# The prompt's first keys, queries and values moved into the last sample's step, small turns spread over the quanta, and h turned one part earlier

## The chip, the core and the metric

One core of one Trainium2 chip runs the whole program. The metric is the device time of one execution in microseconds; lower is better. TensorE does the matmuls and, against an identity, the transposes ("turns"). VectorE and ScalarE read its results out of PSUM, GpSimd and SyncE start transfers.

## What is computed

Two layers, each over 512 prompt rows (one stream) and 128 sample rows (8 streams of 16 rows with 256 cached rows each). From the reference, cut:

```python
z = rmsnorm(h, ln_in) @ w_in
c_q, c_kv, k_r, g_a, u_val, u_gate, g_c = split(z)
q = rmsnorm(c_q, ln_q) @ w_q_b ; ckv = rmsnorm(c_kv, ln_kv) ; kr = rope(k_r)
q_lat = q_nope @ w_uk
o_lat = softmax(q_lat . ckv + q_rope . kr) @ ckv      # 8 heads; prompt: block-causal; samples: with their cache
y_a = rmsnorm((o_lat @ w_uv) * silu(g_a), ln_out_a)
u = u_val * sigmoid(u_gate) ; v = causal_dwconv(u, 31 taps)
y_c = rmsnorm(silu(layernorm(v)) * silu(g_c), ln_out_c)
h = h + concat(y_a, y_c) @ w_out
h = h + sigmoid(rmsnorm(h, ln_pg) @ w_pg) * (p @ w_pe)
```

A final rmsnorm ends the trunk. All is fp32.

## The kernel before

**Tiles and parts.** The rows are five token tiles of 128, t = 0 to 3 the prompt's and t = 4 the samples'. A dense product is made of parts, each a slab of weight rows. A part's weights come as raw pieces (WR); ScalarE's `high(i)` (L937) rounds them to WHI, VectorE's `low(i)` (L1279) forms WLO, what WHI lacks. `high(i)` first waits until TensorE is through with part i-2, whose place it takes. A **quantum** (L583) is one part on one tile: two halves, and each half three matmuls (WHI on the tile's high half, WLO on it, WHI on its low half) into `acc[t]`, the bank of PSUM that the tile has. Each layer has the parts u0 (numbers 0 to 3), zA (4 to 7), u1 (8 to 11), ga (12 to 15), gc (16 to 19), oa0 and oa1 (20 to 23), oc0 and oc1 (24 to 27), pg0 (28 to 31), pg1 (32 to 35).

**Shared banks.** All that isn't a dense product goes through three other banks, S, T and O. `shared_bank_plan` (L99) gives each its users in a fixed order, mostly in turn (`cyc`). TensorE's `fill_wait` (L307) holds a user until the one before it in its bank is drained by ScalarE or VectorE.

**Order.** Each engine's program is written out in order: `tensor_layer` (L527), `scalar_layer` (L918), `vector_layer` (L1266), GpSimd's (L1620) and SyncE's (L447). In a layer TensorE runs u0 (with the turns of the tap weights, of w_uk, of the conv states and of the embeddings in two blocks), zA, u1 with the latents' turns (`turn_latents`, L654) and the samples' queries (`sample_queries` L664, qs0 and qs1; `latent_queries` L673, ql0 and ql1), ga's first part, then eight **sample steps** s (scores, probabilities' turn `flip_probs`, values, the cache's turn `flip_cache` L715). Between those stand halves of ga and gc, as many a step as `FILL` says. Then come the prompt's first keys, queries and value rows, and 32 **units** u (eight heads of four query blocks i; `scores` L794, `values` L805), again with halves from `FILL`. After them follow the dense oa, oc and pg. `NEXT_PART` names the step at whose start ScalarE and VectorE split the next part.

**VectorE's taps.** The convolution's 124 taps a layer (L1346, L1349: one tap over 5 x 128 columns) are dealt out over places by `TAP`; they fill VectorE between drains.

**Around h.** oc0 (24, 25) and oc1 (26, 27) give the two column halves of the new residual H; `onto_residual` (L1527, adds in L1534) waits for `acc[t]` and adds. `flip_half(("h", t, k))` turns H of tile t, half k; ScalarE and VectorE split what is turned (L1289, XLO in L1295), and pg0 needs it.

## Time and profile before

| | |
|---|---|
| median of 3 runs | 858.03 us (857.94 to 858.8) |
| profiled execution | 859.08 us |
| its span, first to last instruction | 857.3 us |
| granted TensorE clock, mean | 0.979 |
| busy: TensorE, VectorE, ScalarE, GpSimd | 791.9, 572.9, 410.4, 67.9 us |
| chain that ended last | PE 84%, ACT 8%, DVE 5%, issue 2%, DMA 1% |

Times in the rows below count from the span's start. PE is TensorE, PEld its weight loads, DVE VectorE, ACT ScalarE, POOL GpSimd. A row of a timeline has the start, the duration of the group of like instructions (x their number), and in brackets the idle time before and who ended it. The granted clock is 1.00 at 2.4 GHz and 0.50 at 1.2 GHz; between those, a stretch has some of both.

### The profile page before, as it was taken

To read this page: it belongs to the slowest core of one execution; us is meant where nothing else is said; L and a number is where in the kernel's file an instruction comes from. 1 tells how busy PE (TensorE), PEld (TensorE's weight loads), DVE (VectorE), ACT (ScalarE), POOL (GpSimd) and SP (SyncE) were. 2 spreads that over 40 slices of the span, in tenths; PEclk is the share of its full clock that TensorE was granted. 3 is DMA by queue.
4 is the path that set the end of the run, shared out by engine and by line. 5 is a ranking of instruction groups with operands and counts; after the bars stand their busy time and mean duration, and the time that the engine had idled before them with its cause. 6 is when DMAs were issued, how large, how long until landed. Compare 5 with 4: busy or idle time off the path is not lost.

```text
span 857.3 us, 10488 instructions
## 1 busy us (share of the span) xinstructions
PE 791.9 (92%) x3782; PEld 612.0 (71%) x3782; DVE 572.9 (67%) x1093; ACT 410.4 (48%) x944; POOL 67.9 (8%) x104
## 2 busy tenths in 40 slices
PE   6999999889998899989999999998999889998992
PEld 5789878556766578868888878774767556886881
DVE  3337968879893885355463687888989478645455
ACT  3655554544345562244365474565334557313544
POOL 5000124000000420000000012210000030000000
PEclk9999999989999999999999999999999999998997
DMA  9522222010000163312172222211000003331203
GB/s 301 175 75 69 69 67 84 25 50 24 5 22 1 35 199 112 124 51 92 55 258 65 74 75 84 55 55 30 21 26 24 1 24 137 117 117 33 92 1 122
DMA packets 40569, 65.26 MB, mean 76 GB/s; under 512 B 7774, under 2 KB 19898, under 8 KB 40502
## 3 DMA queue, kind: packets, MB, share of 16 engines
q1 hardware_dynamic: 37354, 58.45, 21.7%
q0 software_dynamic: 3104, 6.12, 2.5%
q8 instruction: 31, 0.51, 0.2%
q14 instruction: 20, 0.16, 0.1%
q10 hardware_dynamic: 60, 0.02, 0.0%
HBM read 57.86 MB, written 7.17 MB: 76 GB/s over the span
## 4 chain that ended last, share of the span: by engine, by line
PE 84%; ACT 8%; DVE 5%; issue 2%; DMA 1%; SPq 0%; DVEq 0%; ACTq 0%
PE acc L598 18%; PE acc L600 17%; PE acc L599 17%; PE sharedT L532 6%; PE sharedS L802 4%; PE sharedT L791 4%; PE acc L711 4%; PE sharedO L814 3%; ACT JUNK L928 2%; PE sharedT L785 2%; ACT WHI L932 2%; PE sharedO L532 1%; PE sharedS L532 1%; DVE WLO L1285 1%; ACT KH L932 1%
## 5 line engine op out<-in xcount | busy, mean ns | idle before, releaser
L598 PE MATMUL acc<-WHI,XHI 128*128 128x512 f32 (+1 forms) x720 | 311.8, 433 | 11.4 <-DVE H L1534 8.2
L600 PE MATMUL acc<-WHI,XLO 128*128 128x512 f32 (+1 forms) x720 | 280.8, 390 | 0.0
L599 PE MATMUL acc<-WLO,XHI 128*128 128x512 f32 (+1 forms) x720 | 280.4, 389 | 0.0
L1349 DVE SCALAR_TENSOR_TENSOR VT<-UX,CWT,VT 128x640 f32<-128x640 f32 x240 | 211.8, 883 | 5.3
L1285 DVE SCALAR_TENSOR_TENSOR WLO<-WR,GT,WHI 128x512 fp32r<-128x512 f32 (+1 forms) x144 | 100.1, 737 | 104.6 <-ACT WHI L932 104.5
L598 PEld LDWEIGHTS acc<-WHI,XHI 128*128 128x128 f32 x720 | 137.1, 190 | 42.5 <-issue 14.7
L599 PEld LDWEIGHTS acc<-WLO,XHI 128*128 128x128 f32 x720 | 137.2, 191 | 29.1 <-issue 6.0
L600 PEld LDWEIGHTS acc<-WHI,XLO 128*128 128x128 f32 x720 | 136.6, 190 | 27.1
L932 ACT ACTIVATE WHI<-WR,GT 128x512 fp32r<-128x512 f32 (+1 forms) x144 | 94.8, 708 | 114.0 <-PE acc L600 108.8
L932 ACT ACTIVATE PT<-sharedT 128x384 f32<-128x384 f32 (+1 forms) x80 | 35.9, 448 | 76.3 <-PE sharedT L532 76.2
L814 PEld LDWEIGHTS sharedO<-V,PT 128*128 128x128 f32 x320 | 44.2, 191 | 19.5 <-issue 14.6
L802 PE MATMUL sharedS<-KH,QH 128*128 128x128 f32 (+3 forms) x128 | 47.5, 453 | 5.9 <-DVE NBIAS L1403 3.7
L814 PE MATMUL sharedO<-V,PT 128*128 128x128 f32 x320 | 47.5, 279 | 1.4 <-ACT PT L932 1.4
L1120 ACT ACTIVATE SB<-SB,NBIAS 128x384 f32<-128x384 f32 (+1 forms) x80 | 45.5, 569 | 4.6 <-DVE NBIAS L1403 4.6
L928 ACT ACTIVATE JUNK<-H 128x512 bf16<-128x512 f32 (+1 forms) x50 | 40.2, 803 | 8.2 <-DVE H L1499 4.0
L532 PE MATMUL sharedT<-IDENT,SB 128*128 128x128 f32 x208 | 36.4, 275 | 5.4 <-ACT KH L932 4.2
L711 PE MATMUL acc<-WR,PTR 128*128 128x512 f32 x80 | 37.3, 593 | 0.0
L1403 DVE CUSTOM_DVE_ANT_0 SB<-sharedS,MASK 128x128 f32<-128x128 f32 (+1 forms) x64 | 31.0, 485 | 8.3 <-PE sharedS L802 7.8
L791 PE MATMUL sharedT<-CQT,WQ 128*128 128x512 f32 x64 | 33.3, 647 | 1.4 <-ACT KH L932 1.4
L1009 ACT ACTIVATE TH<-acc,HR 128x512 f32<-128x512 f32 x40 | 27.2, 685 | 12.2 <-PE acc L600 9.0
L532 PEld LDWEIGHTS sharedT<-IDENT,SB 128*128 128x128 f32 x208 | 25.0, 141 | 9.8 <-issue 7.8
L1652 POOL TENSOR_TENSOR VT<-VT,CTK 128x512 f32<-128x512 f32 x10 | 13.5, 1347 | 230.0 <-DVE VT L1455 230.0
(191 smaller groups left out, 857.8 us busy)
## 6 DMA issues: line engine op xcount, KB each, us to landing
WR<-in_w_in_dram SPq DMA_DIRECT2D x32, 256.0 KB, 3.0
WR<-in_w_in_dram SPq DMA_DIRECT2D x16, 512.0 KB, 3.6
WR<-in_w_out_dram SPq DMA_DIRECT2D x16, 512.0 KB, 3.7
WR<-in_w_pg_dram SPq DMA_DIRECT2D x16, 512.0 KB, 3.5
WR<-in_w_in_dram SPq DMA_DIRECT2D x8, 416.0 KB, 3.7
residual_spill<-H SPq DMA_DIRECT2D x5, 512.0 KB, 3.4
H<-residual_spill SPq DMA_DIRECT2D x10, 256.0 KB, 3.4
H<-in_x_prompt_dram SPq DMA_DIRECT2D x4, 512.0 KB, 8.1
```

Source lines behind the costliest of these rows:

```text
L532: return nc.tensor.transpose(out, in_, IDENT[0:rows, 0:rows])
L598: mm(out, hi, w_hi, start=(first and k == 0), stop=False)
L599: mm(out, hi, w_lo, start=False, stop=False)
L600: last = mm(out, lo, w_hi, start=False, stop=(final and k == 1))
L711: last = mm(acc[t][:, :], PTR[:, k, P * t:P * (t + 1)], WR[:, j % RAW, k, :], start=(k == 0), stop=(k == 1))
L791: last = mm(bank((l, name))[:, :], WQ[:, k, h, :], CQT[:, k, 0:SEQ], start=(k == 0), stop=(k == 1))
L802: fill_inc(mm(bank((l, name))[:, 0:w], QH[:, h % 2, P * i:P * (i + 1)], KH[:, h % 2, 0:w], start=True, stop=True), (l, name))
L814: last = mm(quad(name)[:, i, :], PT[:, n % 2, j, :], V[:, j, P * (h // 2):P * (h // 2 + 1)], start=(j == 0), stop=(j == i))
L928: av(JUNK[:, 0:src.shape[-1]], src, ACT.Square, scale=scale * n ** -0.5, accum_out=MS[:, col:col + 1]).then_inc(squares, 1)
L932: return av(out, in_, ACT.Copy) if scale is None else av(out, in_, ACT.Copy, scale=scale)
L1285: out = stt(out=WLO[at_k], in0=raw[:, k, :], scalar=gain_column(i, k), in1=WHI[at_k].bitcast(F32), op0=ALU.mult, op1=ALU.subtract)
L1349: ins = stt(out=out, in0=src, scalar=w, in1=out, op0=ALU.mult, op1=ALU.add)
```

## The change

- **h.** TensorE turns half 0 of tile t of H behind oc1's first part instead of its second; VectorE makes low(27) behind the fourth add of oc0 and the low halves of h between the adds.
- **Preparation of the prompt.** keys(0), queries(0) and value rows 0 and 1 stand in sample step 7, between its halves; the values of sample 7, value rows 2 and 3 and the turn of u's last columns stand behind, between four halves called prep. The samples' head outputs (`oa`) come in unit 0. `FILL` gives 4 halves to each sample step and to prep, then 1, 2, 2, 0 to a head's four units. `TAP` follows. In a step, ScalarE and VectorE now split the next part after the gates, not before.
- **Small turns.** Those of w_uk, the states and the embeddings stand one by one behind quanta of parts 2 and 3, those of u's first columns behind quanta of zA's part 2.
- **Latents.** The sample tile's comes first; twelve quanta of u1 run before them, not ten. qs0's matmuls stand behind the third latent, qs1's behind the fifth, ql0's and ql1's two quanta later, the cache's first turn one more quantum later. high(10) and low(10) stand ahead of the latents' scaling.
- **GpSimd** waits in layer 0 for the last tile of x and the last raw piece at the start before it loads the caches.

The functions `turn_small` and `turn_embeddings` are cut into single turns with the same matmuls. The rest of the diff, cut:

```diff
-for _n, _m in enumerate([4, 4, 4, 4, 4, 4, 3, 3] + [1, 1, 2, 2] * HEADS):
+for _n, _m in [*((n, 4) for n in range(NB)), ("prep", 4), *((NB + u, (1, 2, 2, 0)[u % 4]) for u in range(UNITS))]:
...
-    TAP[_n] = _take(3 + _n % 2)
-TAP["turn"] = _take(8)
+    TAP[_n] = _take((3, 3, 4, 4, 4, 4, 3, 3)[_n])
+TAP["turn"] = _take(6)
 for _u in range(UNITS):
-    TAP[NB + _u] = _take(2 + _u % 2)
+    TAP[NB + _u] = _take((3, 3, 4, 1)[_u % 4])
+LATENT_TILES = [TILES - 1, *range(TILES - 1)]
...
-        for t in range(TILES):
+        for t in LATENT_TILES:
             cyc((l, ("small", t)))
-        cyc(*((l, n) for n in ("qs0", "qs1", "ql0", "ql1")))
+            if t == LATENT_TILES[2]:
+                cyc((l, "qs0"))
+            if t == LATENT_TILES[4]:
+                cyc((l, "qs1"))
+        cyc((l, "ql0"), (l, "ql1"))
         order["T"] += [(l, ("c", 0)), (l, ("c", 1))]
...
-            order["T"].append((l, ("p", s)))
-        order["T"] += [(l, ("k", 0)), (l, ("q", 0))]
-        for j in range(4):
-            cyc((l, ("v", j)))
-        cyc(*((l, ("u", 3, part)) for part in range(2)))
-        order["S"].append((l, "oa"))
+            if s < NB - 1:
+                order["T"].append((l, ("p", s)))
+        order["S"] += [(l, ("v", 0)), (l, ("v", 1)), (l, ("s", NB)), (l, ("u", 3, 0))]
+        order["T"] += [(l, ("k", 0)), (l, ("q", 0)), (l, ("p", NB - 1)), (l, ("v", 2)), (l, ("v", 3))]
+        order["O"] += [(l, ("u", 3, 1)), (l, "oa")]
         for u in range(UNITS):
             h, i = divmod(u, 4)
-            order["S"].append((l, ("s", NB + u)))
+            if u:
+                order["S"].append((l, ("s", NB + u)))
...
-            turn_small()
-            for c in (2, 3):
-                for t in range(TILES):
-                    copied_wait(pe, (l, ("x", t, 1)))
-                    quantum("u0", c, t)
-                if c == 2:
-                    turn_embeddings()
+            turn_taps()
+            for t in range(TILES):
+                copied_wait(pe, (l, ("x", t, 1)))
+                quantum("u0", 2, t)
+                if t < 2:
+                    turn_key_weights(t)
+                elif t < 4:
+                    turn_state(t - 2)
+            for t in range(TILES):
+                quantum("u0", 3, t)
+                if t < 3:
+                    turn_embeddings(t)
             for c in range(4):
                 for t in range(TILES):
                     quantum("zA", c, t)
-                if c == 1:
-                    turn_u(0)
-                    turn_u(1)
+                    if c == 2 and t in (1, 3):
+                        turn_u(t // 2)
...
-            for c in range(2):
-                for t in range(TILES):
-                    quantum("u1", c, t)
+            rest = [("u1", c, t) for c in range(4) for t in range(TILES)] + [("ga", 0, t) for t in range(TILES)]
+            def go_on(n):
+                for _ in range(n):
+                    quantum(*rest.pop(0))
+            go_on(12)
             pe.wait_ge(latents_ready, l + 1)
-            for t in range(TILES):
...
                 turn_latents(t)
-                quantum("u1", 2, t)
...
+                go_on(1)
+                if n == 2:
+                    pe.wait_ge(wq_rot, 2 * (l + 1))
+                    pe.wait_ge(wq_in, 32 * (l + 1))
+                    copied_wait(pe, (l, ("small", TILES - 1)))
+                    sample_queries(0)
+            sample_queries(1)
+            go_on(2)
             copied_wait(pe, (l, "uk0"))
             copied_wait(pe, (l, "uk1"))
-            for t in range(TILES):
-                quantum("u1", 3, t)
-                if t == 0:
-                    copied_wait(pe, (l, ("small", TILES - 1)))
-                if t in (0, 2):
-                    sample_queries(t // 2)
+            latent_queries(0)
+            latent_queries(1)
+            go_on(1)
...
-            for t in range(TILES):
-                quantum("ga", 0, t)
-                if t == 1:
-                    latent_queries(0)
-                    latent_queries(1)
-                if t == 2:
-                    flip_cache(0)
-            copied_wait(pe, (l, "ql1"))
-            sample_scores(0)
-            flip_cache(1)
...
-            keys(0)
-            queries(0)
-            sample_values(NB - 1)
-            for j in range(4):
...
-            turn_u(3)
-            fill_wait(pe, (l, "oa"))
-            copied_wait(pe, (l, ("o", NB - 1)))
-            for h in range(HEADS):
-                last = mm(bank((l, "oa"))[:, VH * h:VH * (h + 1)], OL[:, h, :], WKV[:, h, NOPE:P], start=True, stop=True)
-            fill_inc(last, (l, "oa"))
-            for j in range(4):
-                copied_wait(pe, (l, ("v", j)))
+            if l == 0:
+                pe.wait_ge(tables_in, 16 * 2)
+                pe.wait_ge(const_set, 10)
+            flip_cache(0)
+            go_on(2)
+            copied_wait(pe, (l, "ql1"))
+            sample_scores(0)
+            flip_cache(1)
+            go_on(3)
+            for s in range(NB):
+                if s < NB - 1:
+                    sample_scores(s + 1)
+                filler(s, slice(0, 1))
+                if s:
+                    sample_values(s - 1)
+                if s < NB - 2:
+                    flip_cache(s + 2)
+                if s == NB - 1:
+                    value_rows(0)
+                    keys(0)
+                    filler(s, slice(1, 2))
+                    value_rows(1)
+                    queries(0)
+                    filler(s, slice(2, None))
+                else:
+                    filler(s, slice(1, None))
+                if s in (0, 1):
+                    turn_u(2, (s,))
+                pe.wait_ge(p_scaled, NB * l + s + 1)
+                flip_probs(s, PAST + P)
             scores(0)
+            filler("prep", slice(0, 2))
+            sample_values(NB - 1)
+            value_rows(2)
+            filler("prep", slice(2, None))
+            turn_u(3, (0,))
+            value_rows(3)
+            turn_u(3, (1,))
...
                 filler(NB + u, slice(0, 1))
+                if u == 0:
+                    sample_heads()
+                    for j in range(4):
+                        copied_wait(pe, (l, ("v", j)))
...
-                    if c == 1:
+                    if c == 0:
...
+            high(first_i + 10)
             act.wait_ge(rstd_ready, RSTDS * l + 2)
-            for t in range(TILES):
...
-            high(first_i + 10)
-            for t in range(TILES):
...
-                if t == 1:
+                if t == 0:
                     high(first_i + 11)
...
-                if n in NEXT_PART:
-                    high(first_i + NEXT_PART[n])
...
+                if n in NEXT_PART:
+                    high(first_i + NEXT_PART[n])
...
+            low(first_i + 10)
             dve.wait_ge(rstd_ready, RSTDS * l + 2)
...
-                if n in NEXT_PART:
-                    low(first_i + NEXT_PART[n])
...
+                if n in NEXT_PART:
+                    low(first_i + NEXT_PART[n])
...
+                else:
+                    taps(TAP[s][:2])
+                    queries_out(0)
+                    taps(TAP[s][2:])
...
             low(first_i + 26)
             for t in range(TILES):
                 onto_residual("oc0", t)
-            low(first_i + 27)
-            for t in range(TILES):
-                low_half((l, ("h", t, 0)))
+                if t == 3:
+                    low(first_i + 27)
+                if t > 1:
+                    low_half((l, ("h", t - 2, 0)))
+            low_half((l, ("h", 3, 0)))
+            low_half((l, ("h", 4, 0)))
             low(first_i + 28)
...
+                pool.wait_ge(x_in[TILES - 1], 16)
+                raw_wait(pool, RAW - 1)
```

On VectorE at the end of oc0, layer 0: the adds to H, the splits of weights (WLO) and of turned H (XLO). Before:

```order
L1285 SCALAR_TENSOR_TENSOR WLO<-WR,GT,WHI 128x512 x4
L1534 SCALAR_TENSOR_TENSOR H<-acc,RS,H 128x512 x5
L1285 SCALAR_TENSOR_TENSOR WLO<-WR,GT,WHI 128x512 x2
L1295 TENSOR_TENSOR XLO<-sharedS,XHI 128x512
L1295 TENSOR_TENSOR XLO<-sharedT,XHI 128x512
L1295 TENSOR_TENSOR XLO<-sharedO,XHI 128x512
L1295 TENSOR_TENSOR XLO<-sharedS,XHI 128x512
L1295 TENSOR_TENSOR XLO<-sharedT,XHI 128x512
L1285 SCALAR_TENSOR_TENSOR WLO<-WR,GT,WHI 128x512 x2
L1534 SCALAR_TENSOR_TENSOR H<-acc,RS,H 128x512 x5
```

and changed:

```order
L1579 SCALAR_TENSOR_TENSOR H<-acc,RS,H 128x512 x3
L1334 TENSOR_TENSOR XLO<-sharedS,XHI 128x512
L1579 SCALAR_TENSOR_TENSOR H<-acc,RS,H 128x512
L1324 SCALAR_TENSOR_TENSOR WLO<-WR,GT,WHI 128x512 x2
L1334 TENSOR_TENSOR XLO<-sharedT,XHI 128x512
L1579 SCALAR_TENSOR_TENSOR H<-acc,RS,H 128x512
L1334 TENSOR_TENSOR XLO<-sharedO,XHI 128x512
L1334 TENSOR_TENSOR XLO<-sharedS,XHI 128x512
L1334 TENSOR_TENSOR XLO<-sharedT,XHI 128x512
L1324 SCALAR_TENSOR_TENSOR WLO<-WR,GT,WHI 128x512 x2
L1579 SCALAR_TENSOR_TENSOR H<-acc,RS,H 128x512 x5
```

Two XLO now stand between the adds of oc0 and three behind low(27), where before all five followed it.

On VectorE at the samples' queries, layer 0 (WLO is low(11), VT are taps, QH the drains of qs0 and qs1). Before:

```order
L1349 SCALAR_TENSOR_TENSOR VT<-UX,CWT,VT 128x5x128 x6
L1285 SCALAR_TENSOR_TENSOR WLO<-WR,GT,WHI 128x512 x2
L1349 SCALAR_TENSOR_TENSOR VT<-UX,CWT,VT 128x5x128 x8
L1391 TENSOR_TENSOR QH<-sharedT,ROPET 128x8x16 x4
L1349 SCALAR_TENSOR_TENSOR VT<-UX,CWT,VT 128x5x128 x2
L1391 TENSOR_TENSOR QH<-sharedO,ROPET 128x8x16 x4
L1285 SCALAR_TENSOR_TENSOR WLO<-WR,GT,WHI 128x512 x2
```

and changed:

```order
L1388 SCALAR_TENSOR_TENSOR VT<-UX,CWT,VT 128x5x128 x6
L1324 SCALAR_TENSOR_TENSOR WLO<-WR,GT,WHI 128x512 x2
L1388 SCALAR_TENSOR_TENSOR VT<-UX,CWT,VT 128x5x128 x8
L1430 TENSOR_TENSOR QH<-sharedO,ROPET 128x8x16 x4
L1388 SCALAR_TENSOR_TENSOR VT<-UX,CWT,VT 128x5x128 x2
L1430 TENSOR_TENSOR QH<-sharedO,ROPET 128x8x16 x4
L1324 SCALAR_TENSOR_TENSOR WLO<-WR,GT,WHI 128x512 x2
```

The order is as it was; both drains now read bank O, where before the first read T.

On TensorE at the end of u1, layer 0 (QH,OL are the latent queries ql0 and ql1; V and CKR the cache's rows). Before, where u1's last quantum ended two quanta of ga ahead of the first row:

```order
L678 MATMUL sharedS<-QH,OL 128x128 x4
L678 MATMUL sharedT<-QH,OL 128x128 x4
L598 MATMUL acc<-WHI,XHI 128x512
L599 MATMUL acc<-WLO,XHI 128x512
L600 MATMUL acc<-WHI,XLO 128x512
L598 MATMUL acc<-WHI,XHI 128x512
L599 MATMUL acc<-WLO,XHI 128x512
L600 MATMUL acc<-WHI,XLO 128x512
L532 MATMUL sharedT<-IDENT,V 128x128
```

and changed, where the quantum between is u1's last:

```order
L688 MATMUL sharedS<-QH,OL 128x128 x4
L688 MATMUL sharedT<-QH,OL 128x128 x4
L604 MATMUL acc<-WHI,XHI 128x512
L605 MATMUL acc<-WLO,XHI 128x512
L606 MATMUL acc<-WHI,XLO 128x512
L604 MATMUL acc<-WHI,XHI 128x512
L605 MATMUL acc<-WLO,XHI 128x512
L606 MATMUL acc<-WHI,XLO 128x512
L538 MATMUL sharedT<-IDENT,V 128x128
```

The cache's turn stood behind the third quantum of ga and now stands straight behind u1's last.

## Rows read from the trace of the kernel before

**Rows 1.** The page's busy times: us, share of the span, instructions.
```profile
PE 791.9 (92%) x3782; PEld 612.0 (71%) x3782; DVE 572.9 (67%) x1093; ACT 410.4 (48%) x944; POOL 67.9 (8%) x104
```

**Rows 2.** TensorE's timeline: start, us, engine, line, operation; [idle before <-releaser].
```profile
101.47 0.48 PE L598 MATMUL acc<-WHI,XHI 128*128 128x512 f32 x1
102.25 0.40 PE L598 MATMUL acc<-WHI,XHI 128*128 128x512 f32 x1
102.94 0.39 PE L598 MATMUL acc<-WHI,XHI 128*128 128x512 f32 x1
...
104.31 1.95 PE L669 MATMUL sharedO<-CQT,WQ 128*128 128x128 f32 x16
```

**Rows 3.** Waits: engine and line, whom for, us, times, longest us.
```profile
PE acc L598 <- DVE H L1534: 8.2, 2, 4.1
```

**Rows 4.** TensorE's timeline at the end of oc1 of layer 0.
```profile
365.60 0.60 PE L532 MATMUL sharedT<-IDENT,H 128*128 128x128 f32 x4
370.31 0.55 PE L598 MATMUL acc<-WHI,XHI 128*128 128x512 f32 x1 [4.11 <-DVE H L1534]
```

**Rows 5.** VectorE's timeline at the same place.
```profile
368.09 1.41 DVE L1285 SCALAR_TENSOR_TENSOR WLO<-WR,GT,WHI 128x512 fp32r<-128x512 f32 x2 [0.53 <-ACT WHI L932]
...
369.42 3.38 DVE L1534 SCALAR_TENSOR_TENSOR H<-acc,RS,H 128x512 f32<-128x512 f32 x5
```

**Rows 6.** Stretches: length, busy PE PEld DVE ACT POOL, granted clock, DMA share, GB/s.
```profile
158.54:187.85 29.31, 23.12 (x80) 13.40 (x79) 21.66 (x34) 13.61 (x32) 1.11 (x2) 0.83 0.11 33
574.64:598.66 24.02, 19.95 (x80) 11.81 (x79) 19.64 (x32) 13.53 (x32) 1.11 (x2) 0.93 0.08 27
370.31:374.00 3.69, 3.69 (x11) 3.00 (x12) 2.48 (x4) 0.06 (x1) 0.00 (x0) 0.54 0.44 142
781.34:787.00 5.66, 5.66 (x15) 4.52 (x16) 3.18 (x5) 0.60 (x1) 0.00 (x0) 0.50 0.29 93
187.85:253.78 65.93, 64.08 (x311) 44.96 (x311) 58.72 (x110) 26.26 (x72) 0.00 (x0) 1.00 0.05 19
```

**Rows 7.** Timelines of ScalarE, TensorE and VectorE at the start and in u0.
```profile
11.69 1.33 ACT L932 ACTIVATE WHI<-WR,GT 128x512 fp32r<-128x512 f32 x2 [1.64 <-DMA WR<-in_w_in_dram]
...
33.21 0.63 PE L532 MATMUL sharedS<-IDENT,VT 120*128 120x120 f32 x4 [1.01 <-ACT OL L932]
...
34.63 1.35 ACT L932 ACTIVATE WHI<-WR,GT 128x512 fp32r<-128x512 f32 x2
...
36.01 1.42 DVE L1285 SCALAR_TENSOR_TENSOR WLO<-WR,GT,WHI 128x512 fp32r<-128x512 f32 x2 [0.72 <-ACT WHI L932]
```

**Rows 8.** TensorE's timeline: idle times of layer 0.
```profile
62.66 0.33 PE L532 MATMUL sharedT<-IDENT,H 128*128 128x128 f32 x1 [1.71 <-ACT UX L932]
...
89.54 0.50 PE L598 MATMUL acc<-WHI,XHI 128*128 128x512 f32 x1 [1.17 <-DVE WLO L1285]
...
121.03 0.88 PE L751 MATMUL sharedS<-CTK,V 128*128 128x384 f32 x2 [0.78 <-ACT CTK L932]
...
163.85 1.07 PE L785 MATMUL sharedT<-CKVT,WKV 128*64 128x512 f32 x2 [1.41 <-ACT PT L932]
```

**Rows 9.** VectorE's timeline, layer 0: taps, then the drain of qs0.
```profile
96.13 4.56 DVE L1349 SCALAR_TENSOR_TENSOR VT<-UX,CWT,VT 128x640 f32<-128x640 f32 x5
...
103.37 0.88 DVE L1391 TENSOR_TENSOR QH<-sharedT,ROPET 128x128 f32<-128x128 f32 x4
```

**Rows 10.** ScalarE's timeline, layer 0: high(13), then the latent queries.
```profile
109.10 1.34 ACT L932 ACTIVATE WHI<-WR,GT 128x512 fp32r<-128x512 f32 x2 [5.12 <-PE acc L600]
...
112.87 0.79 ACT L932 ACTIVATE V<-sharedS 128x128 f32<-128x128 f32 x4
113.76 0.79 ACT L932 ACTIVATE V<-sharedT 128x128 f32<-128x128 f32 x4
```

**Rows 11.** TensorE's timeline: the turn of unit 1's probabilities.
```profile
187.85 0.41 PE L532 MATMUL sharedT<-IDENT,SB 128*128 128x128 f32 x2 [0.35 <-ACT KH L932]
```

**Rows 12.** The page's costliest groups: busy, mean ns; idle before.
```profile
L932 ACT ACTIVATE PT<-sharedT 128x384 f32<-128x384 f32 (+1 forms) x80 | 35.9, 448 | 76.3 <-PE sharedT L532 76.2
```

More of the change, by code:

```diff
@@ L1179, in scalar_layer @@
                 probs(NB + u, P * (i + 1))
+                if u == 0:
+                    filled_wait(act, (l, "oa"))
+                    drain_inc(copy(OTOK[:, TILES - 1, :], bank((l, "oa"))[:, :]), (l, "oa"))
                 if i == 1 and h < HEADS - 1:
@@ L1475, in layer_norm @@
                     normed(n - TILES)
-            queries_out(0)
-            taps("turn")
+            taps(TAP["turn"][:2])
             mask(NB, P, MASK[:, 512 - P:512])
+            taps(TAP["turn"][2:])
+            filler_gate("prep")
             for u in range(UNITS):
@@ L1484, in vector_layer @@
                     mask(NB + u + 1, w, MASK[:, 512 - w:512])
-                taps(TAP[NB + u][:1])
+                first = 2 if i == 2 else 1
+                taps(TAP[NB + u][:first])
                 if i == 0 and h:
@@ L1489, in vector_layer @@
                     queries_out(h + 1)
-                taps(TAP[NB + u][1:])
+                taps(TAP[NB + u][first:])
                 filler_gate(NB + u)
```

101 lines of the change are left out of this document (50 added, 51 removed).

## The prediction

> **What bounds the kernel now.** I read, in this order: the page's busy times, the waits by engine, the timelines of TensorE, VectorE and ScalarE around each idle time of TensorE, and the table of stretches with their granted clock. TensorE is busy 791.9 of 857.3 us [rows 1], so it is the bound, and the change can win or lose only in two ways: in the 65 us in which it idles, and in the stretches in which it runs at the lower of its two clock levels. No matmul of the products is removed. The profiled execution took 859.08 us, 1.05 above the median of 858.03; I sum against 859.08 and take 1.05 off at the end. A quantum (one part of the weights on one token tile, 6 matmuls) is 2 x 0.69 = 1.38 us, by the distance from the first to the fourth matmul, 102.25 to 102.94 [rows 2].
>
> **h turned one part ahead.** TensorE waits 8.2 us in two places, one in each layer, for the residual adds that fill H [rows 3]. The first quantum of pg0 starts at 370.31 after 4.11 us idle [rows 4], because VectorE has the 1.41 us of WLO (part 28) at 368.09 and then the adds of oc1 at 369.42, 3.38 for five, still to do [rows 5]: H's second half is turned late, or rather the first half was, as its low halves stood behind part 28 on VectorE. The change turns tile t's first half while oc1's first part runs, a whole part (5 x 1.38 = 6.9 us) earlier, and VectorE splits it between the adds of oc0. I place part 28's split at 362.65 and H's first low half ahead of it, so pg0 finds all it needs at about 365.9; what is late next there, the adds of oc1, have 5 quanta of cover. Gain 2 x 4.11 = 8.2. Behind both idle times stands a stretch at a granted clock of 0.54 for 3.69 us and of 0.50 for 5.66 us [rows 6], so 3.69 x 0.46 + 5.66 x 0.50 = 4.5 more. **+12.7.** This is the one term with one answer.
>
> **Start.** ScalarE waits 1.64 us for a weight piece at 11.69 [rows 7] while GpSimd's queue loads the caches; these loads now wait for the last tile of x and of the raw pieces. Between 0 and 1.64: **+1.0**. The caches are needed past 115 us, so nothing is late for it.
>
> **Small turns behind quanta (u0).** In layer 0 the 1.01 us idle at 33.21 goes, since ScalarE's copies no longer hold TensorE in one block [rows 7]. But ScalarE's high(3) and with it VectorE's low(3) still follow the copies of the state, and the state's second turn now stands behind tile 3 of part 2, with one quantum of cover before part 3 needs the split. From the turn's end: the copies, 0.6 us, then 34.63 to 36.01 + 1.42 = 37.43, 2.8 us [rows 7], less 1.38 of cover: 2.0 us of a new stall in each layer. Behind the third embedding turn the same happens to part 4 with more cover, 0.5. A first half behind a turn takes 0.78 (101.47 to 102.25), not 0.69 [rows 2], so some six more switches cost 0.5. Together 3.0 a layer, less 1.01 in layer 0: **-5.0**.
>
> The page "TensorE: Matmul & The Clock Gate" of the Trainium skill (Step-by-step: what each phase is for) says that the weights of the next tile load while this tile's matmul runs; by it a switch would cost nothing, and the 0.5 a layer would be 0. The row's 0.78 beside 0.69 speaks for a small price, so I keep it.
>
> **From zA to ga (the latents).** Three idle times go: 1.71 at 62.66, behind turn_u's two turns in a block, 1.17 at 89.54, behind low(10), and 0.78 at 121.03 [rows 8]; layer 1 has them alike. That is 3.7 a layer. Three come:
> First, low(8) stands behind the taps of z7, some 0.65.
> Second, qs0 and qs1, which were in two shared banks, are now in the same (O in layer 0), so the second block of queries waits until VectorE has drained the first. VectorE has low(11) and then eight taps in front of that drain: they end 96.13 + 7.24 = 103.37, where the drain starts and takes 0.88 [rows 9]. The latents start two quanta later than before but without the 1.17 idle, so low(11) comes some 1.1 us later and the drain ends at about 105.35, in the time of the trace before. TensorE gets to qs1, which stood at 104.31 [rows 2], after 17 quanta instead of 18, that is at 104.31 - 1.38 - 1.17 = 101.8 on the same scale. Stall 3.5.
> Third, the cache turn of sample 0 now comes straight behind the last quantum of u1, and its bank T is that of ql1 (layer 0) or follows ql0's place (layer 1). ScalarE's copy of ql1 stands behind high(13), and that waits for u1's last quantum: 109.10 high(13), three tiles of u, 112.87 ql0, 113.76 ql1, end 114.55 [rows 10]. In before two to three quanta of ga lay over these 5.45 us; now none does. With the usual 0.35 from a ScalarE copy to the matmul [rows 11] it is 5.8 us in layer 0 and, one copy of 0.89 less, 4.9 in layer 1. The three cost 9.95 and 9.05, less 3.7 each. **-11.6.** From both sides: if the queues of VectorE and ScalarE run ahead by as much as TensorE does, the two stalls may be as low as 1.5 and 3.5 a layer (then -4 for the term); above, 1 us more each.
>
> **The clock behind the new idle times.** Before, both idle times of 4.11 us were followed by a stretch at the lower level, which gave away 1.7 and 2.8 us [rows 6]; the stretch of layer 0 with idle times of 1.41 [rows 8] has 0.83 on average. A layer now has idle times of 3.5 and 5.8 within some 12 us. One fall for each is 1.7 to 2.8, so 3.5 a layer when the two overlap in part; another 1.5 in all for the 2.0 us ones of u0. **-8.5**, bounds 0 and -14.
>
> **Prompt's first keys, queries, values in sample step 7, and the units.** The stretch from the turn of sample 6's probabilities to that of unit 1's takes 29.31 us in layer 0, of which TensorE is busy 23.12 at a clock of 0.83, and 24.02 in layer 1, with 19.95 busy at 0.93 [rows 6]. At full clock the same work is about 18.7 (19.95 less the 1.3 that the lower level cost). The changed kernel has seven more halves done by then (4 in each of steps 6, 7 and prep, then 1 and 2, against 3, 3, none, 1 and 1): 7 x 0.69 = 4.8. Idle remains of 1.0 (the copies behind gates, and the turned u before scores(1)). That is 24.5 in either layer: +4.8 and -0.5. In the units VectorE has 11 taps a head, not 10, 0.88 each, and the fourth unit of a head has no half over its wait: its probabilities' copy (ScalarE, mean 0.448) [rows 12] and the exponentials lie bare, some 0.6. Five heads took 65.93 with TensorE at 64.08 [rows 6]; they get 5 halves less (3.5) and wait 5 x 0.6 more at least: 65.75, +0.2 a layer. The halves run out in the same head, which leaves +1.5 a layer for the units behind it. **+6.5 and +1.2, so +7.7.** Bounds: +2 and +12.
>
> **Sum.** 12.7 + 1.0 - 5.0 - 11.6 - 8.5 + 7.7 = -3.7, so 862.8 in the profiled execution's scale, 861.7 as a median.
>
> **Rivals.**
> The clock doesn't fall. The same stalls, without the 8.5: 853.2. For it: TensorE ran at 1.00 through all of the five heads with their many idle times of 0.35 [rows 6, 11]. Against it: both places with 4.11 were followed by the lower level.
> One of the bank waits is hidden. If TensorE is held earlier by another wait, the drain of qs0 is done when it gets there: 2 x 3.5 less and half of the clock's term (4.2) with it, 850.5. It decides at VectorE reaching the drain 3.5 us earlier than I place it. Against it: the eight taps in front are in the order as before.
> VectorE becomes the bound in the units. It is busy 58.72 of 65.93 us in five heads [rows 6]; with one more tap a head 63.1 of 65.75. If more than 2.6 us of its old waits stay beside that, the units get slower: with all 7.2 of them, 70.3 for five heads, 4.5 lost, 12 over both layers, 873; with half, 867.
> That the change doesn't do what it says: the shared banks have an order fixed by a plan, so a turn that is moved ahead on TensorE may wait there for its bank. For h that would leave the 8.2 where they are: 870 in all. Bank and order around h are the same three in turn as before, so I give it little.
>
> **How the numbers follow.** Forecast, 858 to 865.5: 0.48. Clock stays: 0.22, 850 to 856. One bank wait hidden: 0.14, 848.5 to 855. VectorE in the units: 0.11, 866 to 873. h not moved, or something else slower: 0.05. A measurement of this kernel can tell 0.2% (1.7 us) from no change, so "same" is 856.3 to 859.7. Of the forecast's 0.48, 0.10 lies there and none below. Faster 0.22 + 0.14 = 0.36; same 0.10 and 0.02 from elsewhere, 0.12; slower 0.52. Range 850.5 to 866.5: it takes in the forecast and most of the two faster cases and leaves out VectorE's.
>
> **What would show it.** The wait of TensorE for the residual adds gone, and full clock behind both places: h right. An idle time of TensorE before the second block of sample queries, released by VectorE's drain, and one of 5 to 6 us before the first cache turn, released by ScalarE's copy of the latent queries: the bank waits right; without them, wrong, and the time then below 856. Granted clock in the 10 us behind these: below 0.7 for the clock's term. An idle time of 2 us at u0's last part: the small turns right. The turn of unit 1's probabilities some 24 us behind that of sample 6: the prep right. VectorE over 95% busy in the five heads with TensorE waiting for its masks: the third rival.

## The result and the profile after

The changed kernel takes 868.77 us (median of 4 runs, 867.72 to 869.52), the kernel before 857.99 beside it: a ratio of 1.0124, 95% interval 1.0107 to 1.0142. It is slower, by 10.8 us where 3.7 were forecast, and the time lies above the range that was given. The profiled execution took 868.33 us with a span of 866.5; the mean granted clock is 0.977, against 0.979.

To see where the time went I cut both traces at the same places of the program: the turn of the tap weights in u0, the first turn of latents, the turns of the probabilities of samples 0 and 6 and of units 1 and 21, and the first turn of y. Each stretch is the difference of two starts in TensorE's timeline. In the changed kernel two quanta (2.76 us) stand ahead of the latents that stood behind them before, so the second and third line are also given without that shift.

| stretch | before, layer 0 / 1 | changed, layer 0 / 1 | difference | forecast |
|---|---|---|---|---|
| start to tap weights' turn | 30.36 | 28.60 | -1.8 | -1.0 |
| tap weights to latents, shift taken out | 57.41 / 56.25 | 60.5 / 60.4 | +3.1 / +4.2 | +1.7 / +2.7 |
| latents to sample 0's probabilities, same | 38.29 / 38.27 | 48.8 / 48.7 | +10.5 / +10.4 | +10.8 / +9.9 |
| sample 0's probabilities to unit 1's | 61.79 / 56.49 | 56.57 / 56.59 | -5.2 / +0.1 | -4.8 / +0.5 |
| five heads, unit 1 to unit 21 | 65.93 / 66.15 | 67.00 / 67.00 | +1.1 / +0.9 | -0.2 / -0.2 |
| unit 21 to y | 45.73 / 45.74 | 45.12 / 45.12 | -0.6 / -0.6 | -1.5 / -1.5 |
| y to next layer's tap weights; y to the end | 148.14 / 146.75 | 142.25 / 139.85 | -5.9 / -6.9 | -5.8 / -6.9 |

The sum of the differences is +9.2 before rounding, that of the spans too. The forecast's clock term stands in the stretches that it spoke of. The distance between the medians, 10.8, is larger than 9.2 because the profile of the kernel before ran 1.1 above its median and that of the changed kernel 0.4 below.

TensorE's idle times in the changed kernel, from its timeline (start, duration, engine, line, operation; in brackets the idle time and who ended it):

```profile
39.95 0.50 PE L604 MATMUL acc<-WHI,XHI 128*128 128x512 f32 x1 [2.04 <-DVE WLO L1324]
...
50.57 0.46 PE L604 MATMUL acc<-WHI,XHI 128*128 128x416 f32 x1 [0.69 <-DVE WLO L1324]
...
75.40 0.50 PE L604 MATMUL acc<-WHI,XHI 128*128 128x512 f32 x1 [0.87 <-DVE WLO L1324]
...
106.49 3.47 PE L679 MATMUL sharedO<-CQT,WQ 128*128 128x128 f32 x16 [3.50 <-DVE QH L1430]
...
121.60 0.45 PE L538 MATMUL sharedT<-IDENT,V 128*128 128x128 f32 x1 [5.32 <-ACT V L964]
...
542.33 0.33 PE L538 MATMUL sharedT<-IDENT,V 128*128 128x128 f32 x1 [4.44 <-ACT V L964]
```

The idle times of [rows 8] at 62.66, 89.54 and 121.03 are gone. In their place stand 2.04 and 0.69 at u0's last part and zA's first, 0.87 in zA, 3.50 ahead of the second block of sample queries and 5.32 (layer 1: 4.44) ahead of the cache's first turn. Behind the long ones the clock falls. Stretches of the changed kernel (length, busy PE PEld DVE ACT POOL, granted clock, DMA share, GB/s):

```profile
39.95:44.00 4.05, 4.05 (x14) 3.31 (x15) 0.00 (x0) 0.66 (x2) 0.00 (x0) 0.66 0.36 105
106.49:109.90 3.41, 3.41 (x17) 3.41 (x18) 1.62 (x2) 0.00 (x0) 0.00 (x0) 0.56 0.00 0
121.60:127.00 5.40, 5.40 (x16) 4.45 (x17) 2.28 (x3) 0.60 (x1) 3.55 (x8) 0.54 0.40 103
171.51:194.49 22.98, 21.58 (x99) 14.09 (x98) 19.42 (x31) 12.88 (x31) 1.11 (x2) 1.00 0.20 65
194.49:261.49 67.00, 62.20 (x297) 42.49 (x296) 61.33 (x113) 27.99 (x74) 0.00 (x0) 1.00 0.05 16
```

At 0.66, 0.56 and 0.54 the first three gave away 1.4, 1.5 and 2.5 us; in layer 1 the same three places gave away 1.7, 2.7 and 1.7. The fourth, from sample 6's probabilities to unit 1's, now runs at full clock (before 29.31 us at 0.83, [rows 6]). The fifth is the five heads: TensorE is busy 1.9 us less than in [rows 6], and the stretch is 1.1 longer.

The queues behind the two bank waits, first VectorE's, then ScalarE's timeline of the changed kernel:

```profile
96.99 1.42 DVE L1324 SCALAR_TENSOR_TENSOR WLO<-WR,GT,WHI 128x512 fp32r<-128x512 f32 x2 [2.92 <-ACT WHI L964]
...
105.56 0.88 DVE L1430 TENSOR_TENSOR QH<-sharedO,ROPET 128x128 f32<-128x128 f32 x4
```

```profile
116.38 1.33 ACT L964 ACTIVATE WHI<-WR,GT 128x512 fp32r<-128x512 f32 x2 [10.56 <-PE acc L606]
...
119.90 0.77 ACT L964 ACTIVATE V<-sharedS 128x128 f32<-128x128 f32 x4
120.53 0.82 ACT L964 ACTIVATE V<-sharedT 128x128 f32<-128x128 f32 x4
```

low(11) ends at 98.4, then come the eight taps, and the drain of qs0 starts at 105.56; the matmuls of qs1 start when it ends. high(13) starts at 116.38, when u1's last quantum is through, and ql1's copy ends at 121.35, 0.25 ahead of the cache's turn.

Where H is turned, TensorE no longer waits. The last turn of half 0 now stands behind oc1's first part, the second part of oc1 follows (five quanta), and pg0's first matmul starts 0.22 us behind oc1's last, where [rows 4] have 4.11 us of idle time. The granted clock from 366.27 to 378 is 1.00.

```profile
365.91 0.60 PE L538 MATMUL sharedT<-IDENT,H 128*128 128x128 f32 x4
...
372.98 0.39 PE L606 MATMUL acc<-WHI,XLO 128*128 128x512 f32 x1
373.20 0.39 PE L604 MATMUL acc<-WHI,XHI 128*128 128x512 f32 x1
```

### The profile page after: what moved, and what is told of

It is laid out like the page before. It is cut to its first block, busy times and chain, and to the rows that moved or that the text cites. A ratio compares the mean times of both kernels' runs of the same rounds, so it can differ in the third digit from the quotient of the medians.

```text
span 866.5 us, 10496 instructions
## 1 busy us (share of the span) xinstructions
PE 793.1 (92%) x3782; PEld 613.0 (71%) x3782; DVE 571.2 (66%) x1093; ACT 413.1 (48%) x944; POOL 68.0 (8%) x104
## 4 chain that ended last, share of the span: by engine, by line
PE 74%; DVE 17%; ACT 6%; issue 1%; DMA 1%; SPq 0%; DVEq 0%; ACTq 0%
PE acc L604 17%; PE acc L606 16%; PE acc L605 16%; DVE VT L1388 10%; PE sharedT L538 5%; PE acc L727 4%; PE sharedO L806 3%; PE sharedS L794 2%; DVE WLO L1324 2%; ACT WHI L964 2%; PE sharedS L538 1%; PE sharedO L538 1%; DVE SB L1442 1%; PE sharedT L783 1%; PE sharedS L767 1%
## 5 line engine op out<-in xcount | busy, mean ns | idle before, releaser
L604 PE MATMUL acc<-WHI,XHI 128*128 128x512 f32 (+1 forms) x720 | 315.8, 439 | 8.4 <-DVE WLO L1324 7.2
L1579 DVE SCALAR_TENSOR_TENSOR H<-acc,RS,H 128x512 f32<-128x512 f32 x40 | 28.6, 745 | 4.9 <-PE acc L606 3.6
L1363 DVE SCALAR_TENSOR_TENSOR H<-TH,H 128x512 f32<-128x512 f32 x20 | 13.6, 689 | 25.1 <-ACT TH L1041 24.9
```

Of the source, the lines that this page charges most:

```text
L604: mm(out, hi, w_hi, start=(first and k == 0), stop=False)
```

## The experiments

The theory at this point: h and the preparation do what was forecast; the loss is made by waits that other parts of the change bring with them (the shared bank of the sample queries, the cache's turn straight behind u1, the small turns one by one), each with the clock behind it, and by the units, where VectorE's taps (eleven a head) take what fewer halves should give. The rival: the engines' queues only pass the lateness on, so that a wait taken away comes back at the next place. All comparisons below are with the kernel before on the same chip; stretches are from the profiled executions.

**h alone.** The kernel before with only this:

```diff
-                    if c == 1:
+                    if c == 0:
                         flip_half((l, ("h", t, 0)), H[:, t, :])
...
-            low(first_i + 27)
-            for t in range(TILES):
-                low_half((l, ("h", t, 0)))
+                if t == 3:
+                    low(first_i + 27)
+                if t > 1:
+                    low_half((l, ("h", t - 2, 0)))
+            low_half((l, ("h", 3, 0)))
+            low_half((l, ("h", 4, 0)))
```

> The kernel before with the part on h alone (half 0 of H turned during oc1's first part, its low halves between the adds of oc0). If the gain of h is local and complete, both waits of 4.11 us go and with them the two stretches at the lower clock: 12.7 us less, 845.3, and nothing else moves. Rival: the next thing late there (VectorE's adds of oc1, or the split of the next part) takes up part of it, and the gain is 5 to 9 us, 849 to 853.

Measured: 843.04 us, ratio 0.9836 (0.9808 to 0.9864). The two stretches behind y lose 5.9 and 6.9 us, to 142.26 and 139.83: the gain of h is whole and local. Another 1.6 us in each layer came in the stretch from sample 6 to unit 1, where no instruction moved: in layer 1 this execution held full clock there and the profile of the kernel before didn't (0.93, [rows 6]), and in layer 0 the clock was 0.88 against 0.83. So the distance to the forecast (14.7 us measured, 12.7 forecast) is in part the clock's, not h's.

**The second block of sample queries in the next bank.** The changed kernel with:

```diff
             if t == LATENT_TILES[4]:
+                turn[0] += 1
                 cyc((l, "qs1"))
```

> The changed kernel with the second block of sample queries in the next shared bank. If it waits only for its bank, the idle time of 3.5 us a layer ahead of it goes, and the lower clock behind it (1.5 in layer 0, 2.7 in layer 1); the latent queries may then wait 0.5 to 1 us for VectorE's drain of the second block. Some 9 us less than the changed kernel, 860. Rival: the eight taps ahead of the drain hold the latent queries as long as they held the bank, and less than 3 us are won.

Measured: 857.37 us, ratio 0.9998 (0.9986 to 1.0010), some 11 us less than the changed kernel. The 3.5 us are gone in both layers, the stretch from the latents on is 39.97 and 40.47 (before the edit 46.04 and 45.91), and the clock stays up between these queries and the cache's turn. The latter still waits, longer in layer 1, since the banks behind have moved one on:

```profile
117.33 0.45 PE L539 MATMUL sharedT<-IDENT,V 128*128 128x128 f32 x1 [4.64 <-ACT V L965]
...
530.35 0.47 PE L539 MATMUL sharedT<-IDENT,V 128*128 128x128 f32 x1 [5.12 <-ACT V L965]
```

It is 4.64 where T is ql0's bank and 5.12 where it is ql1's: which copy the turn waits for goes by the bank. The latent queries now wait 0.50 and 0.49 us for VectorE's drain of the second block, as expected.

**The cache's first turn later.** The changed kernel with:

```diff
-            flip_cache(0)
-            go_on(2)
+            go_on(3)
+            flip_cache(0)
+            go_on(2)
             copied_wait(pe, (l, "ql1"))
             sample_scores(0)
             flip_cache(1)
-            go_on(3)
```

> The changed kernel with the cache's first turn three quanta of ga later, where it stood before. If that turn only waited for ScalarE's copies behind u1's last quantum, the idle times of 5.3 and 4.4 us go and the lower clock behind them (2.5 and 1.7): 14 us less, 855. Rival: the scores then wait for the cache's copy (0.8 at the second in the kernel before) and 11 us are won.

Measured: 856.42 us, ratio 0.9985 (0.9967 to 1.0003). The stretch is 40.61 and 39.84, 5.4 and 6.1 less. What is late next, TensorE's timeline of this kernel:

```profile
123.36 0.33 PE L538 MATMUL sharedT<-IDENT,V 128*128 128x128 f32 x1 [1.05 <-ACT V L964]
...
129.28 0.88 PE L767 MATMUL sharedS<-CTK,V 128*128 128x384 f32 x2 [0.78 <-ACT CTK L964]
```

Three quanta cover all but 1.05 of the copies (0.37 in layer 1), and the scores' wait of 0.78 is the one of the kernel before ([rows 8], 121.03). The two stretches gained 11.5 us together: here the rival was right on the size.

**Both.** The two edits together.

> The changed kernel with both: the second block of sample queries in the next bank and the cache's first turn three quanta later. If the two waits are independent, the stretch from the latents to the first probabilities, 46.0 and 45.9 us, loses the 6.1 and 5.4 of the one and the 5.4 and 6.1 of the other: 34.5 a layer, some 23 less than the changed kernel, 846. Rival: with both gone the latent queries or the first scores wait for VectorE or ScalarE instead, and the stretch stays at 37 to 38, 850.

Measured: 849.33 us, ratio 0.9899 (0.9882 to 0.9915), stretches 35.33 and 36.01. The single gains (6.1 and 5.4; 5.4 and 6.1) add up to 11.5 and 11.5, and 10.7 and 9.9 came. The missing 0.8 and 1.6 aren't a wait. The wait of the latent queries for VectorE's drain is the one that the first edit alone already brought:

```profile
110.90 1.13 PE L689 MATMUL sharedO<-QH,OL 64*128 64x128 f32 x8 [0.48 <-DVE QH L1431]
```

TensorE's idle time in the stretch adds up to within 0.02 us: 3.7 and 3.5 less by the single edits and 7.2 by both in layer 0; 2.3, 3.3 and 5.6 in layer 1. What doesn't add up is the clock. It gave away 4.0 and 4.4 us there in the changed kernel and 1.5 to 1.6 a layer with either edit alone, by one remaining fall; with both it is 1.00 all through. So each edit alone won 2.4 to 2.9 us of clock, and both together only the 4.0 and 4.4 that there were.

The lateness isn't passed on: the two waits were independent, and together they are 20.6 of the 28.2 us that the two stretches up to sample 0's probabilities lost in both layers.

**The small turns in blocks.** The changed kernel with the calls of u0 as before (first block: w_uk twice, states twice; second: the three of the embeddings).

> The changed kernel with the small turns of u0 in two blocks again. If spreading them caused the idle times of 2.04 and 0.7 us a layer at u0's last part and zA's first, these go with the lower clock behind the first (1.4 to 1.7 each layer), and 1.0 us comes back in layer 0 in the middle of the block: 7 us less, 862. Rival: the split of that part is late by VectorE's or ScalarE's other work and the idle times stay: no difference to the changed kernel.

Measured: 860.08 us, ratio 1.0026 (1.0016 to 1.0037), 8 us less than the changed kernel. The stretch to the latents is 59.32 and 58.10 instead of 63.28 and 63.17. The idle times of 2.04 and 0.7 are gone, and 1.01 is back in layer 0.

**One quantum more of cover for the states' turn.** In a kernel with the two waits and the taps mended (below, "combined"), the small turns spread again, but the state's a quantum earlier:

```diff
-                if t < 2:
-                    turn_key_weights(t)
-                elif t < 4:
-                    turn_state(t - 2)
+                if t == 0:
+                    turn_key_weights(0)
+                    turn_key_weights(1)
+                elif t < 3:
+                    turn_state(t - 1)
```

> The combined kernel with the small turns of u0 spread again, but the state's turns one quantum earlier each (both of w_uk behind the first quantum, the state's behind the second and third). If the 2.04 us stall is the copies and the split of part 3 less one quantum of cover, two quanta of cover leave 0.7 us, the clock stays up, and the stretch to the latents takes 59 to 60 us a layer against 63.2 in the changed kernel and 59.3 and 58.1 in the combined: 837. Rival: the state's copies aren't what delays the split (it waits for its buffer), and the stall stays at 2.0: 843.

Measured: 839.37 us, ratio 0.9780 (0.9762 to 0.9798). 1.36 of the 2.05 is gone, one quantum, and the clock stays up:

```profile
40.81 0.50 PE L605 MATMUL acc<-WHI,XHI 128*128 128x512 f32 x1 [0.69 <-DVE WLO L1326]
...
49.81 0.45 PE L605 MATMUL acc<-WHI,XHI 128*128 128x416 f32 x1 [0.70 <-DVE WLO L1326]
```

That settles the cause of the 2.04: the state's copies ahead of high(3), with one quantum of cover. The time is 2.9 us above the combined kernel's, more than the 837 expected. In layer 1 the stretch is 60.19 against 58.10 with blocks; 1.39 are the two idle times, and 0.7 are left for five more places at which a turn stands between quanta, 0.14 each. The Trainium skill's statement ("TensorE: Matmul & The Clock Gate", Step-by-step: what each phase is for), that the next tile's weights load while this one's matmul runs, would make these free; the measured price is small, but not nothing.

**Ten taps a head.** The changed kernel with:

```diff
-TAP["turn"] = _take(6)
+TAP["turn"] = _take(8)
...
-    TAP[NB + _u] = _take((3, 3, 4, 1)[_u % 4])
+    TAP[NB + _u] = _take((2, 3, 2, 3)[_u % 4])
...
-                first = 2 if i == 2 else 1
+                first = 1
```

The last pair is a part of the change that the diff and the list under "The change" leave out: in a head's third unit VectorE does two taps, not one, ahead of its drain of the next head's queries. So this run undoes three things at once: the number of taps, their deal over the four units, and how many stand ahead of that drain.

> The changed kernel with the taps dealt as before: eight instead of six in the preparation and 2, 3, 2, 3 instead of 3, 3, 4, 1 in a head's units. If VectorE's eleven taps a head bind the units, five heads lose most of 5 x 0.88 = 4.4 us of their 67.0 and end at 63 to 64, 6 to 7 less in all, some 862. Rival: the wait in the fourth unit, which has no half, binds them, and the five heads stay at 66 to 67.

Measured: 863.79 us, ratio 1.0072 (1.0056 to 1.0088). The five heads take 64.85 and 64.83, 2.2 less, where 3 to 4 were expected. VectorE's busy time in them falls by 1.7 us (61.33 to 59.62), not by the 4.4 of five taps. The two deals share out nearly the same number of taps over all the units, 56 a layer in the changed kernel and 54 here; eleven a head only run out sooner, and the stretch holds 51 of them there and 50 here by the traces.

**Six halves a head, eleven taps.** The changed kernel with 1, 1, 2, 2 for 1, 2, 2, 0 in `FILL`.

> The changed kernel with 1, 1, 2, 2 halves in a head's units instead of 1, 2, 2, 0. If VectorE binds the five heads, the five halves more (3.5 us) cost nothing there: they stay at 67 and the units behind lose 3.5, so 7 less in all, 862. Rival: TensorE binds them, the five heads get 3.5 longer, the units behind as much shorter, and the time stays within 1 us of the changed kernel.

Measured: 870.67 us, ratio 1.0150 (1.0132 to 1.0167). The five heads take 70.35 and 70.32, 3.4 more, almost what five halves cost (3.45), and the units behind get only 1.6 shorter (43.56). Neither theory holds: it is not VectorE alone, since then the halves would have been free, and not TensorE alone, since then the taps' old deal would have won nothing. With the kernel before and the combined kernels the table is full (five heads, layer 0, us; each number of taps with its own deal):

| | 10 taps a head | 11 taps a head |
|---|---|---|
| 5 halves a head | 64.84 | 67.00 |
| 6 halves a head | 65.93 (before), 66.60 (combined) | 70.35 |

Who stands in the chain that sets the end of these stretches (shares by line, of the kernel before, the changed, ten taps, six halves):

```profile
by line: PE sharedS L802 16.3%; PE sharedT L791 13.0%; PE sharedO L814 12.9%; PE acc L600 9.5%; PE acc L598 9.5%; PE acc L599 9.4%; PE sharedT L532 9.4%; PE sharedT L785 7.7%; ACT KH L932 4.5%; DVE VT L1349 3.9%; DVE WLO L1285 2.0%; issue 1
```

```profile
by line: DVE VT L1388 44.5%; PE sharedO L806 10.0%; DVE SB L1442 8.3%; PE sharedS L794 6.7%; DVE WLO L1324 5.9%; DVE QH L1467 4.6%; PE sharedT L538 3.4%; PE acc L604 2.7%; DVE OTOK L1491 2.5%; PE acc L606 2.4%; PE acc L605 2.4%; issue 2.0%;
```

```profile
by line: DVE VT L1388 15.6%; PE sharedS L794 14.2%; PE sharedT L783 13.3%; PE sharedO L806 8.9%; PE acc L604 8.3%; PE sharedT L777 7.7%; PE acc L606 6.8%; PE acc L605 6.7%; DVE WLO L1324 6.1%; PE sharedT L538 4.4%; DVE QH L1467 3.2%; issue 
```

```profile
by line: DVE VT L1388 33.6%; PE sharedO L806 9.6%; PE sharedT L538 6.7%; DVE SB L1442 6.5%; PE sharedS L794 6.1%; PE acc L606 5.0%; PE acc L605 4.9%; PE acc L604 4.9%; DVE WLO L1324 3.9%; DVE QH L1467 3.5%; issue 2.7%; PE sharedT L783 2.4%;
```

The taps are 3.9% of the chain before, 44.5% in the changed kernel and 15.6% with ten a head. The new deal of the taps is what put VectorE into the path. That it is their number isn't shown, and the busy times don't explain it. The five heads in layer 1 of the kernel before, in the combined kernel with six halves (below), and with six halves and eleven taps:

```profile
598.66:664.81 66.15, 64.27 (x311) 44.98 (x311) 60.56 (x114) 26.26 (x72) 0.00 (x0) 1.00 0.08 25
181.75:248.35 66.60, 64.27 (x310) 44.98 (x311) 61.53 (x115) 29.70 (x78) 0.00 (x0) 1.00 0.05 17
194.68:265.03 70.35, 65.03 (x310) 45.04 (x311) 62.80 (x115) 29.74 (x78) 0.00 (x0) 1.00 0.05 16
```

VectorE is busy 60.56 of 66.15 us in the first, 92%, and 61.33 of 67.00, again 92%, in the changed kernel. The second has more work than the changed kernel on both engines and is 0.4 us shorter. (Cut at units 5 and 17, VectorE is busy 37.5 of 39.8 us in the changed kernel and 35.8 of 39.4 in the second, so there the share does differ.) The third has 1.3 us more VectorE work than the second (0.8 of TensorE's) and is 3.75 longer. Where its longest wait comes from, TensorE's and VectorE's timelines show:

```profile
256.55 0.52 PE L538 MATMUL sharedT<-IDENT,SB 128*128 128x128 f32 x3 [1.58 <-DVE QH L1467]
```

```profile
254.00 1.80 DVE L1388 SCALAR_TENSOR_TENSOR VT<-UX,CWT,VT 128x640 f32<-128x640 f32 x2
255.72 0.68 DVE L1467 TENSOR_TENSOR QH<-sharedT,ROPET 128x512 f32<-128x512 f32 x1
```

The two taps ahead of the drain hold the bank of the queries, and the turn of the third unit's probabilities waits for it. Waits of this kind sum to 3.1 us in these five heads, 1.0 in the changed kernel and 0.5 in the combined kernel with six halves. No run took the number and the deal apart.

**The same five halves, dealt otherwise.** The combined kernel with 1, 1, 2, 1 for 1, 2, 2, 0.

> The combined kernel with 1, 1, 2, 1 halves in a head's units instead of 1, 2, 2, 0: the same five, one moved from the second to the fourth unit. If the fourth unit's bare wait costs what a half is worth, five heads go from 64.8 to 62.5 to 63, 4 us less in all, 832.5. Rival: a half taken from the second unit bares a wait there, and the five heads stay within 0.5 of 64.8.

Measured: 836.31 us, ratio 0.9747 (0.9731 to 0.9764), the combined kernel's time. The five heads take 65.22 and 65.25, 0.4 more than in the combined kernel, as the rival had it. The fourth unit's missing half is thus not the place of the loss, which was my reading.

**Six halves, ten taps, in the combined kernel.**

> The combined kernel with 1, 1, 2, 2 halves in a head's units, as in the kernel before. With ten taps and six halves the five heads should take what they took before, 65.9, and the units behind them 43.6 instead of 45.1: 0.5 a layer less, 835.4. If the halves were free beside VectorE they would stay at 64.8 and the gain would be 1.5 a layer.

Measured: 835.23 us, ratio 0.9735 (0.9715 to 0.9755). 66.60 and 66.65 for the five heads (65.9 expected), 1.8 more for five halves, and 1.6 less behind: a draw. A half is worth 0.69 us of TensorE and takes 0.35 here.

**Without GpSimd's wait.** The combined kernel with the two waits ahead of the cache loads taken out.

> The combined kernel without GpSimd's wait ahead of the cache loads. By the prediction the loads then take 1 us of the start, 837.4. The starts seen so far, 28.3 to 30.5 us with the wait and 30.3 to 30.4 without it, let expect no difference.

Measured: 835.88 us, ratio 0.9743 (0.9727 to 0.9758). No difference. The start to the tap weights' turn is 29.52 here; with the wait it was 28.32 to 30.84 in the eleven profiles that have it, and 30.30 and 30.36 in the kernels that never had it. The first matmul waits for the conv bias's transfer until some time between 6.25 and 7.25 us in these profiles, whatever the kernel.

**Combined.** The changed kernel with the bank, the cache's turn, the small turns in blocks and the taps as before (ten a head).

> The changed kernel with the bank, the cache's turn, the small turns of u0 in blocks and the taps as before: what stays of the change is h, the preparation in the last sample step, the order of the latents and GpSimd's wait. By the runs so far: 866.5 of span less 23 (both waits), less 7 (the small turns), less 6 (taps) is 830 to 834 in the profile, about 833 as a median; it would beat both kernels and h alone (843). Rival: the three gains overlap in VectorE, which gets its work later in each, and it ends at 838 to 842.

Measured: 836.43 us, ratio 0.9751 (0.9736 to 0.9765): 21 us under the kernel before, 32 under the changed one. The page's first line:

```profile
PE 781.5 (94%) x3782; PEld 606.1 (73%) x3782; DVE 570.2 (68%) x1093; ACT 412.5 (49%) x944; POOL 68.0 (8%) x104
```

Its span of 834.5 is 0.5 above the upper end of what was expected, and the median 3.4 above. Against h alone (841.1) the difference lies in layer 0: from sample 0's probabilities to y it takes 166.59 where h alone takes 171.85. In layer 1 the same stretch is 166.61 against 166.72. Where both run at full clock, the preparation gives 0.1 us; in layer 0 it gives 5.3. Of that some 3.4 is the clock, since h alone falls to the lower level behind its idle times there (0.88 over 27.76 us from sample 6 to unit 1; the kernel before falls too, [rows 6] and 163.85 in [rows 8]). About 2 is idle time that only layer 0 has, 1.90 of it in one wait, in h alone as in the kernel before:

```profile
176.46 2.00 PE L832 MATMUL sharedS<-WKV,OL 128*128 128x64 f32 x16 [1.90 <-ACT UX L932]
```

The rest, 1.1 and 0.3 us, lies ahead of sample 0's probabilities.

## Why the prediction was right and wrong

**h: right.** 12.7 forecast, 12.8 measured in place, and confirmed alone. Both idle times and both stretches at the lower clock went, and nothing was late next.

**From zA to ga: right.** The drain of qs0 was placed 3.5 us too late for TensorE, and the trace has 3.50; the cache's turn at 5.8 and 4.9, and it has 5.32 and 4.44, as ScalarE's chain from high(13) on took 4.97 and not 5.45: its copies stand closer (119.90 and 120.53, against 112.87 and 113.76 in [rows 10]). The clock behind them was put at 3.5 a layer and gave away 4.0 and 4.4. What made this possible was to ask of each moved turn which bank it takes and what stands ahead of that bank's drain on the draining engine.

**Small turns: right in kind, too small.** The stall of 2.0 was 2.04, the other 0.5 was 0.69. The term that was mis-sized is the clock behind a stall of 2 us: I took 1.5 for both layers together, and it cost 1.4 in layer 0 and 1.7 in layer 1. That is 1.6 of the 2.9 us by which these stretches are worse than the sum. Another 0.9 is in the idle times: 0.04 and 0.2 a layer in these two, and 0.87 and 0.80 at the taps of z7, where 0.65 was forecast. The last 0.4 wasn't placed; the switches between turns and quanta, put at 0.5 a layer, cost some 0.7 where the runs show them.

**Preparation: right.** 24.5 us from sample 6 to unit 1 were forecast, with step 6's additional half counted in; that half stands ahead of sample 6's turn, and it is 22.98 plus 1.1 in the steps before. The lower level's price in layer 1 was taken as 1.3; 24.02 us at 0.93 make 1.7, and h alone, at full clock there, has 22.33. The gain in layer 0, 5.2, is the clock's more than the order's: in layer 1 the same edit gave nothing, and the combined kernel beside h alone shows the same.

**Units: wrong, with the sign.** I let the five halves that leave the heads pay in full beside a bare wait of 0.6, and let the eleventh tap cost nothing, since VectorE would be busy only 63.1 of 65.75. The second figure is a slip too: 65.93 less 3.5 and plus 5 x 0.6 is 65.4. VectorE is busy 61.33 of 67.00 and is in the chain all the same. The step that failed is this: the price of the taps was read from VectorE's busy share, and a share below one isn't slack when the work stands between a wait and the drain that another engine needs. The share is 92% in layer 1 of the kernel before too, and there as in layer 0 the taps are only 3.9% of the chain. With the taps dealt as before the five heads are 2.2 us shorter, with six halves 3.75 (70.35 against 66.60). How much of that is the eleventh tap and how much its place stays open. It was my third rival, at 0.11 and with a price of 12 us for both layers; its sign, VectorE over 95% busy, didn't come, but TensorE did wait, 2.0 us for VectorE's masks and 1.0 for its drain of the queries in five heads. Of the 1.7 a layer that were forecast as gain, 0.5 and 0.2 were lost instead, 4.1 us in all.

**Start.** 1.0 forecast, 1.8 seen in this profile, by luck: without the wait the combined kernel takes the same time. The starts scatter by 2.5 us from one profile to the next; no run shows the term, and in the sum it hid 0.8.

**The clock-stays rival** fell with the profile, the rival of one hidden bank wait too: both stood in full. The two terms of 4.1 and 2.9 are what lifted the time out of the range (without either of them it would have been inside, at 864.7 or 865.9); its upper end had been drawn to leave out just the rival that came true in part. Another 1.5 of the 7.1 us between forecast and median is how the two profiles lie to their medians.

What stays open: why a half, worth 0.69 us of TensorE, takes 0.35 us in a head with ten taps (0.2 if one compares with the kernel before) and 0.67 with eleven. The chain shows both engines in it, and the third unit's turn behind the queries' drain is one place where TensorE waits. A run with eleven taps and one ahead of that drain, or with ten dealt 3, 3, 3, 1, would tell the number from the place; none was made. The one attempt at the units (a half moved to the fourth) made it 0.4 slower.

## What to carry to other kernels

When a step is moved in a program with a fixed order of shared banks, write down for each bank user its place before and after, and for each drain what stands ahead of it on the draining engine: both large losses here, 3.5 and 5 us, could be read off that way to a tenth or a half of a microsecond. Undo the parts of a mixed change one by one: this one held 13 us of gain in h and 20 us of loss in two orderings of a line or two each. And when filler work is dealt anew on an engine that is 90% busy, don't read its price from the busy share: ask of each piece which drain it now stands ahead of and who waits for that drain, and price it as exposed until a row shows what hides it.

## What the runs showed of the hardware

An idle time of TensorE of 2.04 to 2.05 us stands at the same place of both layers in six of the profiles. Behind eight of the twelve the granted clock fell, to 0.61 to 0.68 over the next 4 to 5 us, at a cost of some 1.6 us each (the stretch from the tap weights to the latents takes 63.2 us with a fall and 61.6 without); behind four it stayed at 1.00, in the same part of the program. Two of them, layer 1 with the bank mended and layer 0 with six halves:

```profile
455.08:460.00 4.92, 4.92 (x26) 4.08 (x27) 0.00 (x0) 1.32 (x4) 0.00 (x0) 1.00 0.30 87
```

```profile
41.80:46.00 4.20, 4.18 (x22) 3.51 (x23) 0.00 (x0) 0.87 (x3) 0.00 (x0) 1.00 0.35 101
```

With 0.69 instead of 2.05 it stayed up in both layers. So one profile's clock behind a stall of this length is one draw (it fell in eight of twelve), and a stretch may differ by 1.6 us between two executions of the same instructions, as the preparation did in h alone.
